# A two-block transformer kernel: the first item behind each seam by token halves, its weights split ahead of the seam, and the gates' sigmoids as tanh

## The reference, cut to what matters

```python
def first_block(x, c, ...):
    mod = c @ w_ada + b_ada                       # six pieces of 1024
    h = modulate(rms_norm(x, g_pre_mix), shift_m, scale_m)
    q_a, k_a, v_a, q_m, k_m, v_m, o_m, i_m, f_m, g_a, g_m = split(h @ w_in)
    y_a = sliding_window_attention(rope(q_a), rope(k_a), v_a)
    y_m = sigmoid(o_m) * head_layer_norm(mlstm(silu(conv(q_m, k_m)), v_m, i_m, f_m))
    merged = sigmoid(g_a) * (y_a @ w_branch_attn) + sigmoid(g_m) * (y_m @ w_branch_mlstm)
    x = x + gate_m * rms_norm(merged @ w_out, g_post_mix)
    h2 = modulate(rms_norm(x, g_pre_ffn), shift_f, scale_f)
    ff = (silu(h2 @ w_ffn_gate) * (h2 @ w_ffn_up)) @ w_ffn_down
    return x + gate_f * rms_norm(ff, g_post_ffn)

def second_block(x, c, ...):
    x = layer_norm(x, emb_ln_g, emb_ln_b)
    sh1, sc1, gt1, sh2, sc2, gt2 = split(silu(c) @ w_ada + b_ada)
    p = (x * (1 + sc1) + sh1) @ w_in              # pu, pv and the columns of RWKV7
    y_a = gelu(pu) * (w_s applied over tokens to layer_norm(gelu(pv)))
    y_b = rwkv7_time_mix(...)
    x = layer_norm(ALPHA * x + gt1 * (concat(y_a, y_b) @ w_out), ln1_g, ln1_b)
    gu = (x * (1 + sc2) + sh2) @ w_ffn_in         # gate and up halves, 2816 each
    f = (silu(gate) * up) @ w_ffn_out
    return layer_norm(ALPHA * x + gt2 * f, ln2_g, ln2_b)
```

## Time and profile before

| | us |
|---|---|
| median of 3 runs | 805.28 |
| lowest, highest | 802.53, 805.87 |
| the profiled execution | 803.44 |
| its span | 801.6 |
| PE busy | 766.2 (96%) |
| DVE busy | 628.1 (78%) |
| ACT busy | 394.6 (49%) |
| POOL busy | 40.7 (5%) |

### The profile page before, as it was taken

The page is one execution under the profiler, slowest core; times in us unless marked ns, Lnnn a source line. Parts: engine busy times, 40 slices in busy tenths (PEclk is TensorE's granted clock), DMA queues, the critical chain, the costliest instruction groups (busy, mean ns, idle before and its releaser), DMA issues.

```text
span 801.6 us, 15845 instructions
## 1 busy us (share of the span) xinstructions
PE 766.2 (96%) x6610; PEld 699.0 (87%) x6610; DVE 628.1 (78%) x811; ACT 394.6 (49%) x558; POOL 40.7 (5%) x61
## 2 busy tenths in 40 slices
PE   4999999889999999999999999999999999999996
PEld 3798888889789999998878987889768999999874
DVE  5869979988988887877868899886697688555447
ACT  3368834765464445443445885532225455445340
POOL 0123000000000000000002000050010000000000
PEclk9999989999999999999999999999999999999998
DMA  9897856764659999998983644500265589666621
GB/s 344 310 326 222 286 196 197 243 224 135 220 172 310 321 309 308 345 319 298 366 267 98 233 115 135 175 4 23 90 233 158 160 274 331 197 196 189 202 84 52
DMA packets 98070, 173.69 MB, mean 217 GB/s; under 512 B 7767, under 2 KB 55230, under 8 KB 97998
## 3 DMA queue, kind: packets, MB, share of 16 engines
q1 hardware_dynamic: 95678, 166.62, 62.7%
q0 software_dynamic: 1872, 5.86, 2.3%
q10 hardware_dynamic: 448, 0.19, 0.1%
HBM read 171.60 MB, written 1.05 MB: 215 GB/s over the span
## 4 chain that ended last, share of the span: by engine, by line
PE 73%; DVE 16%; ACT 5%; DMA 3%; issue 3%; DVEq 0%; SPq 0%; ACTq 0%
PE bank L2129 14%; PE bank L2130 13%; PE bank L2131 13%; PE bank L2402 5%; PE bank L2403 5%; PE bank L2404 5%; PE bank L2104 3%; PE bank L2105 2%; PE bank L2106 2%; DMA raw<-in_w_ada 2%; DVE wlo L473 2%; DVE acc L500 2%; PE bank L2564 1%; ACT whi L694 1%; DVE xn L1566 1%
## 5 line engine op out<-in xcount | busy, mean ns | idle before, releaser
L473 DVE TENSOR_TENSOR wlo<-raw,whi 128x1024 fp32r<-128x1024 f32 (+1 forms) x212 | 254.7, 1214 | 82.9 <-ACT whi L694 79.3
L694 ACT ACTIVATE whi<-raw 128x1024 fp32r<-128x1024 f32 (+1 forms) x212 | 220.0, 1051 | 193.1 <-PE bank L2131 78.4
L2129 PE MATMUL bank<-hh,whi 128*128 128x256 f32 x1016 | 284.2, 280 | 3.0 <-DVE hl L1222 2.9
L2131 PE MATMUL bank<-hh,wlo 128*128 128x256 f32 x1016 | 281.8, 277 | 0.0
L2130 PE MATMUL bank<-hl,whi 128*128 128x256 f32 x1016 | 281.8, 277 | 0.0
L2129 PEld LDWEIGHTS bank<-hh,whi 128*128 128x128 f32 x1016 | 190.7, 188 | 6.2 <-issue 5.6
L2131 PEld LDWEIGHTS bank<-hh,wlo 128*128 128x128 f32 x1016 | 191.8, 189 | 0.0
L2130 PEld LDWEIGHTS bank<-hl,whi 128*128 128x128 f32 x1016 | 190.8, 188 | 0.5 <-issue 0.5
L2402 PE MATMUL bank<-whi,ffh 128*128 128x512 f32 x168 | 65.7, 391 | 0.9 <-DVE wlo L473 0.9
L2403 PE MATMUL bank<-wlo,ffh 128*128 128x512 f32 x168 | 65.4, 390 | 0.0
L2404 PE MATMUL bank<-whi,ffl 128*128 128x512 f32 x168 | 65.4, 389 | 0.0
(11 more groups left out here) (453 smaller groups left out, 1073.9 us busy)
## 6 DMA issues: line engine op xcount, KB each, us to landing
raw<-in_w_ada SPq DMA_DIRECT2D x96, 512.0 KB, 5.3
raw<-in_w_in SPq DMA_DIRECT2D x54, 512.0 KB, 4.6
raw<-in_w_ffn_in SPq DMA_DIRECT2D x88, 256.0 KB, 4.0
raw<-in_w_ffn_gate SPq DMA_DIRECT2D x44, 256.0 KB, 4.6
raw<-in_w_ffn_up SPq DMA_DIRECT2D x44, 256.0 KB, 5.6
raw<-in_w_ffn_down SPq DMA_DIRECT2D x22, 512.0 KB, 5.5
raw<-in_w_ffn_out SPq DMA_DIRECT2D x22, 512.0 KB, 4.3
raw<-in_w_out SPq DMA_DIRECT2D x16, 512.0 KB, 4.0
```

The costliest lines, as they stand in the source:

```text
L473: eng.tensor_tensor(lo[:, 0:nk * width], raw[:, b % RAW, 0:nk * width], hi[:, 0:nk * width].bitcast(fp), ALU.subtract)\
L694: act.activation(weight_place(g)[0][:, 0:nk * width], raw[:, b % RAW, 0:nk * width], ACT.Copy)\
L2129: mm(o, wh[:, k, c], xh[:, kk_, :], start=first, stop=False)
L2131: last = mm(o, wl[:, k, c], xh[:, kk_, :], start=False, stop=end)
```

## The change

**The seams** are worked by token halves. `turn_rows(u, m)` turns the rows of one half; `scale_even` and `round_h` on ACT and `scale_odd` on DVE make `hh` of that half; the low part of the first token half is made by POOL (`first_low`), that of the second by DVE (`second_rows`). The first item behind a seam goes through a new `seam_out`: its result has tokens as rows, in matmuls of 512 columns; for the first token half the products with `hh` run for both halves of the features, and `turn_rows(u, 1)` stands among them. At seam 3 `turn_rows(3, 0)` stands ahead of the last weight block of `wo3b`. At seam 1 twelve filler matmuls are left (`run_on(6)`), at seams 2 and 3 none.

**The first items' weights** are split ahead of the seam and have buffers of their own (`seam_at`). `pv` comes to the place behind seam 2, ahead of `lora`; its four blocks stand among the last blocks of dA (`AMONG_DOWN`). POOL subtracts three of four blocks of `ff0` and all four of `gf0` (`ON_POOL`). With this, gelu(`pv`) and its norm come earlier, and `pu` takes the place that `pv` had.

**The results of ff0 and gf0** have tokens as rows; SiLU and the product are made so, and four transposes in `ff1` and `gf1` (`turn_products`) bring them back.

**The gates:** sigmoid(x) becomes (tanh(x/2) + 1)/2. ACT computes Tanh with a scale of 0.5, DVE's products add 1 in a SCALAR_TENSOR_TENSOR, and the factor 0.5 goes into later operations. `part(3)` moves from seam 1 into `ba1`, and its collection behind the low part of the branches.

```diff
-    middle = ["lora", "k", "r", "v", "pv", "pu", "wo2a", "wo3a", "c21", "wo2b", "wo3b"]
+    middle = ["pv", "lora", "k", "r", "v", "pu", "wo2a", "wo3a", "c21", "wo2b", "wo3b"]
...
+AMONG_DOWN = (("dA9", 0), ("pv", 0), ("pv", 1), ("dA9", 1), ("pv", 2), ("dA10", 0), ("pv", 3), ("dA10", 1))
...
+SEAM = {1: "ff0", 2: "pv", 3: "gf0"}
...
+ON_POOL = {"ff0": (0, 2, 3), "gf0": (0, 1, 2, 3)}
...
+            def first_low(u):
+                for half in range(2):
+                    pool.wait_ge(sem("hh_ready"), 4 * u + half + 1)
+                    x = (slice(None), slice(4 * half, 4 * half + 4), slice(0, P))
+                    pool.tensor_tensor(hl[x], hx[x], hh[x].bitcast(fp), ALU.subtract).then_inc(sem("h_ready"), 1)
...
+            prepare_on(pool, "pool", "ff0")
+            first_low(1)
...
+            prepare_on(pool, "pool", "gf0")
+            first_low(3)
...
+            def scale_even(u, m, half):
+                sh = modT[:, u // 2, (24 if u % 2 else 0):(32 if u % 2 else 8)]
+                n, t = 4 * u + 2 * m + half + 1, slice(m * P, (m + 1) * P)
+                act.wait_ge(sem("gain_ready"), u + 2)
+                act.wait_ge(sem("hx_turned"), n)
+                for k in (4 * half, 4 * half + 2):
+                    ins = act.activation(hx[:, k, t], turned_h(u, k), ACT.Identity, bias=sh[:, k:k + 1],
+                                         scale=gain[:, u, k:k + 1])
+                ins.then_inc(sem("hx_even"), 1)
+            def round_h(u, m, half):
+                n, t = 4 * u + 2 * m + half + 1, slice(m * P, (m + 1) * P)
+                act.wait_ge(sem("hx_even"), n)
+                act.wait_ge(sem("hx_odd"), n)
+                act.activation(hh[:, 4 * half:4 * half + 4, t], hx[:, 4 * half:4 * half + 4, t], ACT.Copy)\
+                   .then_inc(sem("hh_ready"), 1)
+            def make_h(u, m):
+                for half in range(2):
+                    scale_even(u, m, half)
+                    round_h(u, m, half)
...
-                                         b[:, :].rearrange("p (t n) -> p t n", t=2), ACT.Sigmoid)
+                                         b[:, :].rearrange("p (t n) -> p t n", t=2), ACT.Tanh, scale=0.5)
...
+                for name, i in AMONG_DOWN:
+                    split(name, slice(i, i + 1))
...
+            def scale_odd(u, m, half):
+                sh = modT[:, u // 2, (24 if u % 2 else 0):(32 if u % 2 else 8)]
+                dve.wait_ge(sem("hx_turned"), 4 * u + 2 * m + half + 1)
+                for k in (4 * half + 1, 4 * half + 3):
+                    ins = TS(hx[:, k, m * P:(m + 1) * P], turned_h(u, k), gain[:, u, k:k + 1], sh[:, k:k + 1],
+                             ALU.mult, ALU.add)
+                ins.then_inc(sem("hx_odd"), 1)
+            def second_rows(u):
+                for half in range(2):
+                    scale_odd(u, 1, half)
+                for half in range(2):
+                    dve.wait_ge(sem("h_ready"), 4 * u + 2 + half)
+                    dve.wait_ge(sem("hh_ready"), 4 * u + 3 + half)
+                    x = (slice(None), slice(4 * half, 4 * half + 4), slice(P, 2 * P))
+                    TT(hl[x], hx[x], hh[x].bitcast(fp), ALU.subtract).then_inc(sem("h_ready"), 1)
...
-                step(TT(osig[:, m, :], osig[:, m, :], bcs[:, 0, :], ALU.mult))
+                step(STT(osig[:, m, :], osig[:, m, :], 1.0, bcs[:, 0, :], ALU.add, ALU.mult))
...
+            collect_part(3)
+            gains(1, v1T[:, v1["g_pre_ffn"][0]:v1["g_pre_ffn"][1]])
...
-            prepare("lora", slice(0, 1))
-            scale_h(2, first_half=lambda: prepare("lora", slice(1, 2)))
-            prepare("lora", slice(2, 4))
-            prepare("k", slice(0, 2))
+            dve.wait_ge(sem("piece_done"), 10)
             collect_part(8)
             collect_part(9)
+            ln_rows(0, 1)
+            second_rows(2)
+            prepare("lora")
             gains(3, column("ln1_g_2"), b=column("ln1_b_2"))
+            prepare("k", slice(0, 2))
...
+            def turn_rows(u, m):
+                if u == 1:
+                    pe.wait_ge(sem("xn_ready"), 3 + m)
+                    src = xn[:, m * D:(m + 1) * D]
+                else:
+                    pe.wait_ge(sem("xhat_ready"), 2 * u - 3 + m)
+                    src = xt[:, m, :]
+                for k in range(KT):
+                    last = tr(turned_h(u, k), src[:, k * P:(k + 1) * P], ident)
+                    if k % 4 == 3:
+                        last.then_inc(sem("hx_turned"), 1)
+            def seam_out(u):
+                name = SEAM[u]
+                banks = start_item(name)
+                g0 = place[name][1]
+                for m in range(MT):
+                    if m and u == 2:
+                        pe.wait_ge(sem("piece_used"), 10)
+                    t = slice(m * P, (m + 1) * P)
+                    for half in range(2):
+                        n = 4 * u + 2 * m + half + 1
+                        two = (g0 + 2 * half, g0 + 2 * half + 1)
+                        pe.wait_ge(sem("hh_ready"), n)
+                        for g in two:
+                            i, nk, wh, wl = weights(g)
+                            for k in range(nk):
+                                x = hh[:, nk * i + k, t]
+                                mm(banks[m][:, :], x, wh[:, k, :], start=g == g0 and k == 0, stop=False)
+                                mm(banks[m][:, :], x, wl[:, k, :], start=False, stop=False)
+                        if m == 0 and half:
+                            turn_rows(u, 1)
+                        pe.wait_ge(sem("h_ready"), n)
+                        for g in two:
+                            i, nk, wh, _ = weights(g)
+                            for k in range(nk):
+                                last = mm(banks[m][:, :], hl[:, nk * i + k, t], wh[:, k, :], start=False,
+                                          stop=half == 1 and g == two[1] and k == nk - 1)
+                            if m:
+                                last.then_inc(sem("blocks_done"), 1)
...
-            pe.wait_ge(sem(f"pair{place['wo0'][0] % 2}_free"), place["wo0"][0] // 2 + 1)
-            part(3)
-            turn_h(1, lambda m: xn[:, m * D:(m + 1) * D], "xn_ready", 2, 13, 2 * (place["wo1"][0] % 2))
+            turn_rows(1, 0)
+            run_on(6, start_bank("ff0"))
+            def turn_products(n):
+                pe.wait_ge(sem("ffp_ready"), n * (FT // 2) + 1)
+                for m in range(MT):
+                    for f in range(2):
+                        last = tr(bank[6][:, 256 * f + P * m:256 * f + P * m + P],
+                                  ffp[:, 0, 256 * m + P * f:256 * m + P * f + P], ident)
+                last.then_inc(sem("ffp_turned"), 1)
...
-            def seam_parts():
-                run_on(2, 4)
-                part(9, lambda: run_on(4, 4))
-                run_on(1, 4)
-            pe.wait_ge(sem("ln_var"), 1)
             part(8)
-            turn_h(2, lambda m: xt[:, m, :], "xhat_ready", 0, 16, 4, amid=seam_parts)
-            features_out("lora", [0, P, 288 - P], modulated, half_ready=8)
+            turn_rows(2, 0)
+            part(9)
+            seam_out(2)
+            features_out("lora", [0, P, 288 - P], modulated)
...
+                        if m and x and g > g0:
+                            turn_rows(3, 0)
...
-            turn_h(3, lambda m: xt[:, m, :], "xhat_ready", 2, 15, 2 * (place["wo3a"][0] % 2))
```

324 lines of the change are left out of this document (188 added, 136 removed).

## The result

The changed kernel takes 824.97 us (median of 4 runs, 816.42 to 828.09) against 804.2 (4 runs, 802.53 to 805.87): a ratio of 1.0246, interval 1.0188 to 1.0303. It is slower by some 20 us, more than the worst rival allowed (812.2) and outside the range (up to 813). From all medians and ratios here executions over 1.5% longer than the fastest of the same kernel are left out (one of five in run 6, the profiled one, and four of twelve in run 15).

A forecast was written before the change was run, and what follows sets the result against it. PE bounds the kernel, busy 96% of the span with 73% of the last-ending chain. Terms -1.0 - 3.4 + 2.6 - 4.1 + 0.9 + 2.0 + 4.4 = +1.4; 803.44 + 1.4 + 1.84 = 806.7 us, range 798 to 813.

The forecast's parts named there:

- the clock's two falls: Behind seams 2 and 3, granted clock at 0.50 for lack of work on PE: 2 x 2.2 = +4.4 us, bounds 0 to 9.9.
- Moving `pv` ahead of `lora` I cost at nothing.: Lora stretch: no cost, since DVE waits for PE there; without that cover 4 x 1.18 us of subtraction stand open.
- one of my own signs of being wrong: From lora to v: PE waiting for DVE, where the forecast put no cost, would show it wrong.
- the turned products as 0.9 us of PE: In ff1 and gf1: four more transposes each, half a turn of eight, 2 x 0.45 = +0.9 us.
- The forecast of +2.6: End of dA: DVE's eight subtractions in a row finish the last block at 419.15 instead of 416.75; bounds 0 to 3.2.
- My sum lets only such pairs collide.: POOL and DVE delay each other only when both operations have two SBUF inputs; 1.3 us added for meetings at seam 3.
- rival R4: Wider lock: seam 1's single-input L1602 sits out a whole POOL subtraction; +2.1 us, 808.8 in all; chance 0.10.
- +2.0 and a fall of the clock at 2.2: Seam 3: POOL's four gf0 blocks start late behind the broadcasts, +2.0 us (1.6 to 2.4), plus one clock episode.
- as predicted (-3.4): Seam 1: working by token halves, ff0 ends near 246.7 instead of 250.1, a gain of 3.4 us.
- -4.1: Seam 2: fillers and wait go from 9.32 us; two parts and two turns, 5.24 us, stay.
- -2.1: Tanh gates: DVE's waits at L473 go, reaching PE through L2129; with offsets the term is -1.0 (-2.5 to +0.5).
- R3: Slower rival: without fillers the clock falls at all three seams for 3.3 us each, 812.2 in all; chance 0.20.

The follow-up runs named there:

- run 6: Changed kernel with SiLU and product of ff0 ahead of ff1's last weight block on ACT and DVE: 818.74 us, ratio 1.0176.
- run 15: kernel 9 with sixteen filler matmuls before seam 3's first product, without moving the norm of v: 805.89 us, ratio 1.0029.
- run 12: kernel 9 with the two normalisations of v moved back behind the tilde step: 804.13 us, ratio 1.0004.
- run 7: Changed kernel with dA's last four blocks ahead of pv's four instead of among them: 822.44 us, ratio 1.0208.
- runs 1 to 4: Changed kernel, seam 3: POOL's gf0 subtractions before bias fill, 819.9 us; on DVE, 819.63; first-half L1795 as SCALAR_TENSOR_TENSOR, 826.34; gaps between POOL's subtractions, 825.94.
- run 2: Changed kernel with gf0's four subtractions on DVE, none on POOL: 819.63 us, ratio 1.0174.
- run 5: Changed kernel with POOL's third ff0 subtraction held back until the first half of the rows is normalised: 823.4 us, ratio 1.0235.
- run 11: Kernel before with the gates alone changed to tanh, nothing moved: 802.33 us, ratio 0.9971.
- run 10: Kernel before with only the fillers of seams 2 and 3 taken out: 810.55 us, ratio 1.0064.
- kernel 9: Changed kernel with the edits of run 2, run 5, run 6 and run 7 together, plus twelve fillers at seam 2: 805.24 us, ratio 1.0008.
- 12 to 14: kernel 9 with v's norm moved back, 804.13 us; then sixteen fillers at seam 3, 803.64; then also two gf0 blocks on POOL before bias fill, 804.6.
- kernel 13: run 12 plus sixteen filler matmuls before the first product behind seam 3: 803.64 us, ratio 1.0003.

## Why the prediction was wrong

The forecast's terms (us), laid on the stages of the table; `gf0`'s stage is cut at the end of `wo3b`, and the clock's two falls are put where the prediction had them:

| | to wo1's end | seam 1 | ff1 to dA's end | seam 2 | lora to wo3b's end | seam 3 | rest | sum |
|---|---|---|---|---|---|---|---|---|
| forecast | -1.0 | -3.4 | +3.0 | -1.9 | 0 | +4.2 | +0.5 | +1.4 |
| measured | -3.1 | +0.9 | +10.8 | -0.2 | +7.7 | +4.2 | +1.0 | +21.3 |

The measured row adds up to the difference of the spans. The two steps that failed most are terms put at little or nothing: the stage from ff1 to dA's end and the one from lora to wo3b, almost 8 us each. The third is seam 1, by 4.3. From ff1 to dA's end PE waited 7.0 us against 0.4 before, and the clock fell twice, for 3.4 and for 6.8 us; the paragraphs on ff1 and on the end of dA have the two causes.

**"Moving `pv` ahead of `lora` I cost at nothing."** The cover that I named, DVE waiting for PE there, was gone. From the first matmul of lora to wo3b's end PE waited 8.3 us in seven waits against 2.4 in four before, and the clock fell once more, for 3.4 us from 486. The 5.9 us more of waits and half of the fall make 7.6 of the 7.7 us. (The last six matmuls of `wo3b`, 1.4 us, now stand behind the turn; counted ahead of it they end at 616.2, 161.8 us after the first of `lora`; before it was 165.0 with `pv`, 154.1 without.) Of the waits 2.35 us stand at L2628 and 1.55 at L2236, behind `pv`'s norm; run 12 moved the first and removed the second. The other 2.0 us are those at L2741, behind the DVE operation that POOL shut out in the recurrence. I gave a price for the cover's absence (4 x 1.18) and then left it out of the range. PE waiting for DVE in this stretch was one of my own signs of being wrong.

**ff1: no term at all.** I counted the turned products as 0.9 us of PE for the two feed forwards. They made PE wait inside ff1 for a chain of block, SiLU and product, 4.0 us, and a fall of the clock came behind (run 6: the ratio falls by 0.007, 5 to 6 us). I didn't ask what stands ahead of SiLU on ACT.

**End of dA.** The forecast of +2.6 came true in size, as 3.0 us of PE's waits. Their cause was not DVE's eight subtractions in a row, but transfers: ACT waited for each block (run 7). So the number was luck. The fall of the clock there, from 421 to 428, was not in the sum.

**"My sum lets only such pairs collide."** The trace had shown two engines with two operations of two inputs, each longer by about one operation of the other (POOL's were mask operations, not subtractions as I wrote). I took from it 1.3 us for "meetings with DVE" at seam 3. Measured: 9.07 us for an operation of 0.81 (runs 1 to 4). Two things were wrong. The single-input operation is locked out too; that was rival R4, but I priced it at seam 1 only and at one POOL operation (+2.1; there it measured 2.64 against 0.75, +1.9, and PE's wait 3.7). And at seam 3 its wait is for all four of POOL's operations that follow each other, not for one: I had put four of them in a row at just the place where L1795 stands, and had laid only their own length on the path.
The Trainium skill, page "SBUF — State Buffer", section "Who interferes with whom", has the direction right: a DVE operation with two inputs in SBUF contends with a POOL operation that reads SBUF, and one in a 2-port mode contends with POOL, where the first to issue holds the pair "for the whole instruction" and the other "fully blocks". The operations here that read two tiles agree with one instruction's wait (3.44 instead of 1.22 us, 3.46 instead of 1.23); L1795 sat out four instructions in a row, which the page doesn't have.

**Seam 3: the right number by luck.** Forecast were +2.0 and a fall of the clock at 2.2, with PE waiting for POOL's blocks; measured is +4.2 with a fall. But PE waited 8.3 us for DVE and not at all for POOL, whose late start I had made the head of the path. Without POOL's four the stage to gf0's end is 6.8 us shorter (run 2): the seam itself takes 17.8 us there, against 24.5 in the changed kernel and 20.3 before, so it would have given 2.5 us instead of costing 4.2.

**Seam 1.** The mechanism held but for the lock: without it the stage takes 17.2 against 20.4, -3.2 (run 5), as predicted (-3.4). With it, and with the clock's fall behind PE's wait, it is +0.9.

**Seam 2.** -4.1 was nearly right in what it took out: 5.1 us of small work are left ahead of the first product and 0.8 among the products, 5.9 where I had 5.24. But the first product then ran at half clock: -0.2 in all, where with the fall at 2.2 I had -1.9. With fillers put back it is 7.5 (18.4 less 10.9) against 9.3.

**The gates.** -2.1 was right in size: -2.3 us in run 11 (interval 0.5 to 4.3). The way was not: PE's wait of 1.7 us at L2129 stayed, others went.

**The clock.** The size of one fall was about right (2.6 us by run 10, 2.2 predicted), their number was not: behind 200 us six against none, where I had counted two. R3 named this cause, but for lack of fillers only; here waits of PE were followed by falls as well, though not each time. So a wait must be priced with the chance of a fall behind it.

**Why no version beats the kernel before.** With the lock, the queue behind the late block and the order in dA mended, the seams do give what they were meant to: in kernel 9's profile 2.9, 1.8 and 2.3 us, in those of 12 to 14 up to 3.2, 1.8 and 2.5. But from lora to wo3b these kernels take 159.3 to 160.8 us against 154.1 before, 5.2 to 6.7 more, by the waits named above. In 12 to 14 the wider spacing comes on top.

**Still open.** Which operations of DVE a row of POOL operations shuts out, and why DVE and POOL changed order in the recurrence. What the 256-column matmuls' spacing hangs on.

## What to carry to other kernels

Work given to POOL isn't free for DVE: a DVE operation that meets a POOL operation waits for it, and one that reads a single tile waited for four that stood ready in a row, so place them where DVE reads banks or waits, never beside a step that PE waits for. Where PE loses a filler or gains a wait, reckon with half the dense work that may run behind it at half clock (by run 10, 2.6 us for each seam), as a chance and not as a certainty. And where a new step waits inside an item, look at what stands ahead of its producer on each engine before counting it at its own length.

## What the runs showed of the hardware

DVE operations that read one whole tile were shut out by four POOL operations of 2.32 us in a row, and took 9.07 us (TENSOR_SCALAR) and 9.70 us (SCALAR_TENSOR_TENSOR with a column as second input); with gaps between POOL's operations it was 2.33. DVE operations that read two tiles got in behind the first of a row: 3.44 us instead of 1.22 beside the same four, 3.46 instead of 1.23 beside two.

The 256-column matmuls of the feed forward run at one of two spacings, for the same instructions in the same order at full clock. Two windows of the same stage, of kernel 9 and of kernel 13 (PE's count stands in brackets):

```profile
290.00:330.00 40.00, 40.00 (x355) 40.00 (x355) 34.18 (x33) 19.22 (x24) 0.00 (x0) 1.00 0.99 333
```

```profile
290.00:330.00 40.00, 40.00 (x342) 40.00 (x341) 33.32 (x33) 18.10 (x23) 0.00 (x0) 1.00 0.95 321
```

355 against 342 matmuls in 40 us is 0.113 against 0.117 us for each. The kernel before starts at the wider one at 239 and goes over to the denser near 275, and again, 609 and 643, behind seam 3; the changed kernel has the denser from 248 on. The profiles of kernels 6 and 12 to 15 keep the wider one to the end of ff, the others don't. Over ff1 to ff10 the difference is about 4 us, as much as what was looked for here. What chooses it I don't know.
